# A fused decoder layer: the next head group's query, key and value projections moved into the present group's tail, and weight products in two sweeps

## The reference

```python
h = rmsnorm(x, g_pre_mix)
h_q, h_kv, h_pe, z, xbc, dt, gate_a, gate_b = split(h @ w_in)
q = rmsnorm(h_q, g_q) @ w_uq                # 16 heads, 64 + 32 rotary
c_kv, k_pe = rmsnorm(h_kv, g_kv), rope(h_pe)
k, v = c_kv @ w_uk, c_kv @ w_uv             # prompt; rows use the latents
o_attn = softmax(causal(q @ k) * scale) @ v
y, state = ssd_scan(silu(conv(xbc)), dt)    # 32 heads in 8 groups
o_ssm = rms_per_group((y + d_skip * x) * silu(z)) * g_ssm
merged = sigmoid(gate_a) * (o_attn @ w_br_attn) + sigmoid(gate_b) * (o_ssm @ w_br_ssm)
x = x + rmsnorm(merged @ w_out, g_post_mix)
x = x + rmsnorm(square(relu(rmsnorm(x) @ w_up)) @ w_down, g_post_mlp)
```

## Time and profile before

| | |
|---|---|
| median of three executions | 1900.58 us |
| the profiled execution, its own time | 1894.26 us |
| its span, first to last instruction | 1892.5 us |
| TensorE matmuls busy | 1616.1 us (85%), 11520 matmuls |
| VectorE busy | 998.0 us (53%) |
| ScalarE busy | 520.1 us (27%) |
| GpSimd busy | 477.8 us (25%) |
| mean granted TensorE clock | 0.916 of full speed |

### The profile page before, as it was taken

The page is one execution under the profiler, slowest core; times in us unless marked ns, Lnnn a source line. Parts: engine busy times, 40 slices in busy tenths (PEclk is TensorE's granted clock), DMA queues, the critical chain, the costliest instruction groups (busy, mean ns, idle before and its releaser), DMA issues.

```text
span 1892.5 us, 29047 instructions
## 1 busy us (share of the span) xinstructions
PE 1616.1 (85%) x11520; PEld 1391.9 (74%) x11520; DVE 998.0 (53%) x1780; ACT 520.1 (27%) x914; POOL 477.8 (25%) x196
## 2 busy tenths in 40 slices
PE   4788798788887888878876599999999499999995
PEld 4787687676877768777764346464799499999995
DVE  5568688686886868868685412121142622222225
ACT  3232323233232332333322112111222332222221
POOL 1232131221212212122120101111243444444441
PEclk9799899898898988989887799999899699999998
DMA  3132121221212212122130255564232122222221
GB/s 113 45 107 78 37 82 56 73 79 37 82 56 71 80 37 82 57 68 83 37 91 23 74 160 179 161 182 133 86 127 75 34 90 90 92 97 92 90 90 68
DMA packets 115738, 160.51 MB, mean 85 GB/s; under 512 B 18546, under 2 KB 89715, under 8 KB 115603
## 3 DMA queue, kind: packets, MB, share of 16 engines
q1 hardware_dynamic: 53714, 122.21, 20.4%
q10 hardware_dynamic: 61888, 36.44, 7.0%
HBM read 145.87 MB, written 12.74 MB: 84 GB/s over the span
## 4 chain that ended last, share of the span: by engine, by line
PE 60%; DVE 27%; issue 4%; ACT 3%; POOL 2%; DMA 1%; ACTq 1%; SPq 1%; DVEq 0%; POOLq 0%
PE lin L446 38%; PE Pb L664 3%; PE lin L684 3%; POOL w_lo L402 2%; PE Pb L464 2%; PE Pb L666 2%; PE lin L472 2%; DVE csm L1246 1%; DVE sm L1252 1%; DVE arena L1225 1%; PE lin L579 1%; PE Pb L520 1%; DVE acc L1421 1%; DVE arena L1357 1%; PE Pb L561 1%
## 5 line engine op out<-in xcount | busy, mean ns | idle before, releaser
L402 POOL TENSOR_TENSOR w_lo<-w_stage,w_hi 128x1024 fp32r<-128x1024 f32 x184 | 465.8, 2531 | 1365.4 <-ACT w_hi L778 1365.4
L446 PE MATMUL lin<-act_hi,w_hi 128*128 128x260 f32 x1760 | 370.4, 292 | 22.7 <-POOL w_lo L402 10.7
L446 PE MATMUL lin<-act_hi,w_lo 128*128 128x260 f32 x1760 | 358.1, 285 | 0.0
L446 PE MATMUL lin<-act_lo,w_hi 128*128 128x260 f32 x1760 | 357.6, 285 | 0.0
L778 ACT ACTIVATE w_hi<-w_stage 128x1024 fp32r<-128x1024 f32 x184 | 194.0, 1054 | 396.4 <-PE lin L446 366.3
L446 PEld LDWEIGHTS lin<-act_hi,w_hi 128*128 128x128 f32 x1760 | 275.5, 192 | 35.4 <-issue 16.3
L446 PEld LDWEIGHTS lin<-act_lo,w_hi 128*128 128x128 f32 x1760 | 275.9, 192 | 0.0
L446 PEld LDWEIGHTS lin<-act_hi,w_lo 128*128 128x128 f32 x1760 | 275.0, 191 | 0.0
L446 PE MATMUL lin<-mid_hi,w_hi 128*128 128x260 f32 x1024 | 220.0, 298 | 46.0 <-DVE acc L1421 20.8
L446 PE MATMUL lin<-mid_lo,w_hi 128*128 128x260 f32 x1024 | 214.2, 292 | 0.0
L446 PE MATMUL lin<-mid_hi,w_lo 128*128 128x260 f32 x1024 | 213.5, 291 | 0.0
(11 more groups left out here) (227 smaller groups left out, 2234.1 us busy)
## 6 DMA issues: line engine op xcount, KB each, us to landing
w_stage<-in_wall SPq DMA_DIRECT2D x184, 512.0 KB, 3.6
arena<-in_cache ACTq DMA_DIRECT2D x128, 128.0 KB, 2.8
arena<-in_state ACTq DMA_DIRECT2D x16, 512.0 KB, 8.0
out_stateT<-arena ACTq DMA_DIRECT2D x16, 512.0 KB, 4.1
arena<-in_cache SPq DMA_DIRECT2D x64, 128.0 KB, 2.3
o_attn<-in_cache SPq DMA_DIRECT2D x64, 128.0 KB, 2.3
arena<-in_xT SPq DMA_DIRECT2D x8, 520.0 KB, 5.4
out_yT<-arena SPq DMA_DIRECT2D x8, 260.0 KB, 2.0
```

What stands on the lines that cost most here:

```text
L402: pool.tensor_tensor(w_lo[:, slot, :], w_stage[:, slot, :], w_hi[:, slot, :].bitcast(F32), ALU.subtract).then_inc(S["w_split"], 1)
L446: mm = pe.matmul(lin[:, pl.slot, hf, 0:HALF], w[:, ch.slot, off:off + P], r[:, hf * HALF:(hf + 1) * HALF], start=(k == 0 and p == 0), stop ...
```

## The change

Two parts. First, the products uq0, uq1, uk, uv and ql of group i are issued in turn i in place of turn i+1: the queries between the scan and the statistics, keys and values between the statistics and the broadcast, the latent queries behind the broadcast. Turn 0 ends with all of them. ScalarE and VectorE evacuate them there too; `silu(0)` and the second z gate change place on VectorE; the weight chunks and PSUM slots are renumbered (bc, ql, s0 now follow each other, so s0 uses the slot of bc), and `rtmp` lies 16 columns further on. Second, `linear` waits for the high part of the weights alone, does both products with it over all tiles, then waits for the low part and does the third; `between` comes ahead of that second sweep.

```diff
--- before.py
+++ after.py
@@ -46,14 +46,14 @@
 
 
 IN_LIN = ["x0", "x1", "b", "c", "z0", "z1"]
-HEAD_LIN = ["uq0", "uq1", "uk", "uv", "ql", "bB"]
-TAIL_LIN = ["bc"] + [f"s{m}" for m in range(8)]
-FIRST_LIN = IN_LIN
-STEADY_LIN = HEAD_LIN + ["x0", "sA0", "x1", "bC", "sA1", "b", "sA2", "c", "sA3", "z0", "z1"] + TAIL_LIN
-LAST_LIN = HEAD_LIN + ["sA0", "bC", "sA1", "sA2", "sA3"] + TAIL_LIN
-FIRST_CH = IN_LIN
-STEADY_CH = ["UQ", "UKV"] + IN_LIN + ["SA", "SB"]
-LAST_CH = ["UQ", "UKV", "SA", "SB"]
+S_LIN = [f"s{m}" for m in range(8)]
+FIRST_LIN = IN_LIN + ["uq0", "uq1", "uk", "uv", "ql"]
+STEADY_LIN = (["bB", "x0", "sA0", "x1", "bC", "sA1", "b", "sA2", "c", "sA3", "z0", "z1", "uq0", "uq1", "uk", "uv", "bc", "ql"]
+              + S_LIN)
+LAST_LIN = ["bB", "sA0", "bC", "sA1", "sA2", "sA3", "bc"] + S_LIN
+FIRST_CH = IN_LIN + ["UQ", "UKV"]
+STEADY_CH = IN_LIN + ["UQ", "UKV", "SA", "SB"]
+LAST_CH = ["SA", "SB"]
 PRE_LIN = ["bcx", "misc", "q0", "q1", "q2", "kv0", "kv1", "bcq", "bckv"]
 PRE_CH = ["misc", "q0", "q1", "q2", "kv0", "kv1"]
 
...
@@ -432,23 +428,32 @@
 
 
                 if opens:
-                    pe.wait_ge(S["w_split"], ch.index + 1)
+                    pe.wait_ge(S["w_hi_done"], ch.index + 1)
                 free_slot(pl)
                 n = len(offs)
-                first = True
-                for k, (off, (rh, rl)) in enumerate(zip(offs, rhs)):
-                    if between and k == 3 * n // 4:
-                        between()
-                    if rhs_ready:
-                        pe.wait_ge(rhs_ready[0], rhs_ready[1] + (k + 1))
-                    for w, r, p in ((w_hi, rh, 0), (w_hi, rl, 1), (w_lo, rh, 2)):
+
+                def passes(k, of):
+                    off, (rh, rl) = offs[k], rhs[k]
+                    for w, r, p in of:
+                        r = (rh, rl)[r]
                         for hf in range(2):
                             mm = pe.matmul(lin[:, pl.slot, hf, 0:HALF], w[:, ch.slot, off:off + P],
                                            r[:, hf * HALF:(hf + 1) * HALF],
                                            start=(k == 0 and p == 0), stop=(k == n - 1 and p == 2))
-                            if first and opens:
+                            if opens and k == 0 and p == 0 and hf == 0:
                                 open_chunk(ch, mm)
-                            first = False
+                    return mm
+
+                for k in range(n):
+                    if rhs_ready:
+                        pe.wait_ge(rhs_ready[0], rhs_ready[1] + (k + 1))
+                    passes(k, ((w_hi, 0, 0), (w_hi, 1, 1)))
+                if opens:
+                    pe.wait_ge(S["w_split"], ch.index + 1)
+                if between:
+                    between()
+                for k in range(n):
+                    mm = passes(k, ((w_lo, 0, 2),))
                 mm.then_inc(S["lin_done"], 1)
 
             def act_rhs(n=KT):
@@ -508,9 +513,47 @@
                     if has_in:
                         linear(c_lin(i, name), c_chunk(i, name), K8, act_rhs(), between=between)
 
+                def queries():
+                    for h in range(2):
+                        linear(c_lin(i, f"uq{h}"), c_chunk(i, "UQ"), [k * 256 + h * P for k in range(3)],
+                               mid_rhs(0, 3), opens=(h == 0))
+
+                def keys():
+                    linear(c_lin(i, "uk"), c_chunk(i, "UKV"), [0, P], mid_rhs(3, 2))
+
+                def value_rows():
+                    ch, pl = c_chunk(i, "UKV"), c_lin(i, "uv")
+                    free_slot(pl)
+                    for c in range(NCH):
+                        for k in range(2):
...
+                    mm.then_inc(S["lin_done"], 1)
+
+                def latent_queries():
+                    ch, pl = c_chunk(i, "UKV"), c_lin(i, "ql")
+                    free_slot(pl)
+                    pe.wait_ge(S["lin_free"], c_lin(i, "uq1").index + 1)
+                    for k in range(2):
+                        out = lin[:, pl.slot, 0, 16 * k:16 * k + 16]
+                        for n, (w, r) in enumerate(((w_hi, qbd_hi), (w_hi, qbd_lo), (w_lo, qbd_hi))):
+                            mm = pe.matmul(out, w[:, ch.slot, 256 + k * P:384 + k * P], r[:, :],
+                                           start=(n == 0), stop=(n == 2))
+                    mm.then_inc(S["lin_done"], 1)
+
                 if not has_rest:
                     for name in IN_LIN:
                         project(name)
+                    pe.wait_ge(S["act_ready"], KT + 5)
+                    queries()
+                    keys()
+                    value_rows()
+                    latent_queries()
                     return
 
...
@@ -604,7 +620,7 @@
 
                 on_all("bB", 2)
                 pe.wait_ge(S["q_ready"], g * 2 + 2)
-                pe.wait_ge(S["lin_free"], c_lin(i, "uv").index + 1)
+                pe.wait_ge(S["lin_free"], c_lin(i - 1, "uv").index + 1)
                 scores(0)
                 project("x0")
                 for c in range(NCH):
@@ -626,11 +642,18 @@
                     if c < NCH - 1:
                         scores(u + 2)
                     values(u + 1)
+                if has_in:
+                    queries()
                 pe.wait_ge(S["o_ready"], g * 8 + 8)
                 pe.wait_ge(S["sqg_ready"], g * 2 + 2)
                 statistics(Pb[0:TOKT, 2, 0:8], sqg, 2).then_inc(S["g_stat"], 1)
+                if has_in:
+                    keys()
+                    value_rows()
                 pe.wait_ge(S["g_diag"], g + 1)
                 broadcast_stat(c_lin(i, "bc"))
+                if has_in:
+                    latent_queries()
                 for m in range(8):
                     linear(c_lin(i, f"s{m}"), c_chunk(i, "SA" if m < 4 else "SB"),
                            [(m % 4) * P, 512 + (m % 4) * P], mid_rhs(5, 2), opens=(m % 4 == 0),
@@ -866,6 +889,23 @@
                             else d["state"][:, 2 * t:2 * t + 2, :, :]
                         act.dma_start(sS[:, t], src.rearrange("b h p n -> (h p) b n")).then_inc(S[f"st_in{t}"], 16)
 
+                def heads_out():
+                    round_chunk(c_chunk(i, "UKV"))
+                    for h in range(2):
+                        pl = c_lin(i, f"uq{h}")
+                        done(pl)
+                        act.activation(cols(Qt[0:64, h, :]), lin_cols(pl, 0, 64), ACT.Copy)
+                        act.activation(qbd_hi[64 * h:64 * h + 64, 8 * h:8 * h + 8],
+                                       lin[0:64, pl.slot, 1, HALF - NB:HALF], ACT.Copy).then_inc(S["qbd_hi_s"], 1)
+                    pl = c_lin(i, "uk")
+                    round_chunk(c_chunk(i, "UKV").next())
+                    done(pl)
+                    act.activation(cols(Kt[0:64, 0, :]), lin_cols(pl, 0, 64), ACT.Copy).then_inc(S["k_act"], 1)
+                    pl = c_lin(i, "uv")
...
@@ -875,6 +915,7 @@
                     z_evac()
                     conv_tanh(3)
                     finish_inputs()
+                    heads_out()
                     return
 
                 def exponent(u):
...
@@ -1230,6 +1257,39 @@
                     dve.scalar_tensor_tensor(xc[:, k, :], xc[:, k, :], 1.0, cacc[:, k % 2, :], ALU.add, ALU.mult
                                              ).then_inc(S["xc_ready"], 1)
 
+                def queries_out(h):
+                    pl = c_lin(i, f"uq{h}")
+                    done(pl)
+                    link(dve.tensor_tensor(cols(rtmp[64:96, :]), lin_cols(pl, 96, 128), cols(ropet[96:128, :]), ALU.mult))
+                    link(dve.tensor_tensor(cols(Qt[64:96, h, :]), lin_cols(pl, 64, 96), cols(ropet[64:96, :]), ALU.mult))
+                    link(dve.tensor_tensor(Qt[64:96, h, :], Qt[64:96, h, :], rtmp[64:96, :], ALU.add))
+                    dve.wait_ge(S["qbd_hi_s"], i * 2 + (h + 1))
+                    dve.tensor_tensor(qbd_lo[64 * h:64 * h + 64, 8 * h:8 * h + 8],
+                                      lin[0:64, pl.slot, 1, HALF - NB:HALF],
+                                      qbd_hi[64 * h:64 * h + 64, 8 * h:8 * h + 8].bitcast(F32), ALU.subtract
...
@@ -1238,6 +1298,10 @@
                         conv(k)
                     z_gate((0, 1))
                     silu(3)
+                    queries_out(0)
+                    queries_out(1)
+                    keys_out()
+                    latents_out()
                     return
 
                 onehot = ident[0:32, bass.ds(g * 4, 4)]
...
@@ -1394,12 +1428,13 @@
                         conv(c - 1, 1)
 
                 if has_in:
-                    z_gate((0,))
+                    z_gate((0, 1))
+                    queries_out(0)
+                    queries_out(1)
                 dve.wait_ge(S["g_stat"], g + 1)
                 inverse_rms(Pb[0:TOKT, 2, 0:8], 0.25 / (D_INNER // GROUPS), S["g_diag"])
                 if has_in:
-                    z_gate((1,))
-                    silu(0)
+                    keys_out()
```

(8 more changed lines are left out.)

106 lines of the change are left out of this document (33 added, 73 removed).

## The result

The changed kernel takes 1924.22 us in the median of four executions, the kernel before 1898.18 beside it. Over all executions that is a ratio of 1.0147, 95% interval 1.0114 to 1.0181, slower by 1.5% where 0.6% faster was forecast. The profiled execution took 1927.41 us, its span is 1925.6. The first lines of the profile's page show no engine with more work to do: TensorE issues the same 11520 matmuls, and its busy share has not moved. Its busy time has grown with the span: 1639.2 us, where it was 1616.1, at a mean granted clock of 0.909 in place of 0.916.

What follows compares the result with a forecast made beforehand. No engine alone bounds the 119 us turn: TensorE works 102, waiting for VectorE and GpSimd. Seven turns at 1.0, front 3.7 and last head 1.0 give about 12 us won: 1888.6 us, range 1870 to 1903.

Steps and rivals of the forecast that it cites:

- (h): Head, L592 to the scan's L546, 10.85 us in the old kernel: VectorE still needs 10, gain 0.2 (-0.5 to +0.8).
- (d): Inverse root in the tail: GpSimd's low part of SA blocks VectorE for 2 us (0 to 2.5), ending at 478.9.
- (e): Broadcast from 479.0 taking 1.5 us, s0 waiting 0.68 more for its slot: s0 at 483.5, 8.6 later.
- A: The forecast: 5 to 20 us won, moved work mostly given back as the chain to s0 starts later; chance 0.55.
- B: Rival: the tail's hole is filled, the root not blocked or the clock staying up; 1875 us; chance 0.22.
- C: Rival: the move is worth nothing, only the sweeps count; 1894 to 1897 us; chance 0.13.
- D: Rival: between scan and statistics, queries run wholly at 1.2 GHz; 4.4 us a turn lost, 1920 us; chance 0.10.
- The sweeps: In `linear`, waits for GpSimd's low part go: 0.5 us a turn gained, 3.7 (2 to 6) in the front.
- (a): After the scan: uq0 needs z0's PSUM slot, queries stand ahead of statistics, first hole widened from 2.12 to 3.5 us.
- (b): Queries after the scan: 36 matmuls take 5.3 us with a cold start, ending at 470.6 (469.8 to 471.3).
- (c): Statistics behind dense work take 2.02 us, not 3.37, to 472.6; keys and values 4.5 us, to 477.1.
- (f): Output products: VectorE 1.65 us later by the s1 addition, +0.95 beyond s0's delay; s7 ends at 501.6, formerly 492.1.

Runs made afterwards that it cites:

- run a: The kernel before with the new `linear` alone, nothing moved: 1891.47 us against 1894.89, ratio 0.9970.
- run b: The changed kernel with the old `linear`, so the move alone: 1935.29 us, ratio 1.0201 to the kernel before.
- run d: The changed kernel with ScalarE rounding weight chunk SA later, behind the evacuation of the values: 1912.54 us, ratio 1.0088 to the kernel before.
- run f: The changed kernel with statistics and inverse root ahead of the queries and their evacuations: 1916.3 us, ratio 1.0094 to the kernel before.
- run c: The changed kernel with the decoding-state loads issued early, between the two query evacuations: 1909.66 us, ratio 1.0077 to the kernel before.
- run i: The kernel before with its decoding-state loads issued late, behind the evacuation of the values: 1935.56 us, ratio 1.0218 to the kernel before.
- e: The changed kernel with state loads issued early and SA rounded late: 1889.97 us against 1896.88 for the kernel before, ratio 0.9968.
- j: The changed kernel with state loads early, SA rounded late and the old `linear`: 1904.05 us, ratio 1.0038 to the kernel before.
- g: The changed kernel with state loads early, SA rounded late and statistics first: 1906.25 us, ratio 1.0040 to the kernel before.
- k: h with VectorE's convolution halves and `silu` spread among the output products' additions: 1878.35 us against 1895.72 for the kernel before, ratio 0.9897.
- h: The changed kernel reordered: statistics, uq0, broadcast, uq1; keys, values, latent queries between s3 and s4; state loads early; UKV behind SA: 1894.59 us, ratio 0.9975 to before.

## Why the prediction was wrong

The replay was off by 40 us: 12 won were forecast, 28 lost were measured by the ratio (26 by the medians). The step that failed is (h), the head: it gives the loads of the decoding states no price when the projections that cover them are moved away. Two more were mis-sized, the slot of the keys ahead of the broadcast in (d) and (e), and the middle of the turn, which was taken as unchanged.

The cases by name: the forecast A and its rivals B and C fail; D has the sign and, at 1920, nearly the time, but not the mechanism, so its nearness is luck. Its premise, queries and statistics wholly at 1.2 GHz, did not come: the queries took 5.7 us, at a mean granted clock of 0.74, and the statistics 2.00, at 1.00. The stretches are these (columns as in the earlier trace rows):

```profile
471.59:477.30 5.71, 5.71 (x36) 5.71 (x37) 2.35 (x4) 2.36 (x5) 2.38 (x1) 0.74 0.11 14
477.30:479.30 2.00, 2.00 (x35) 2.00 (x34) 1.87 (x5) 0.77 (x2) 0.00 (x0) 1.00 0.62 234
```

The lower end of the range is a small slip: B with the front at its best is 1873, not 1870. By steps:

- **The sweeps** held in the turns: z1's wait is gone in all of them, and run a's seven turns are 4.1 us shorter (3.5 written). The front's 3.7 is not shown: the waits are gone there too, but the first sdm product starts at 145.1 for 146.6, in run a at 146.7, and in run b, without the sweeps, at 144.7.
- **(a), (b), (c)** held: queries at 4.6 us after the scan (4.5 said), 5.7 us long (5.3), statistics 2.00 (2.02).
- **(d)** held, and was the step with the widest bounds: the root is cut by GpSimd for 2.2 us a turn (2 taken), shown by run d. The operation that was cut isn't one of the nine with two inputs that the step counted, but the `tensor_scalar` ahead of them (L1115). By the Trainium skill, page "SBUF — State Buffer", section "Who interferes with whom", the block was certain for an operation with two inputs; the trace of run f agrees, where L1118 took 2.23 us. But the step left out that the broadcast takes the slot of uk: it waits for VectorE's copy at L1278 too, 0.88 us more (486.54 for 485.66), since `keys_out` comes behind the root.
- **(e)** was right in the sum and wrong in its terms: the broadcast took 2.07 us for 1.5, and the 0.68 us for the slot did not come: s0 starts at 490.95, while the pair of subtractions at 490.10 runs to 491.47. That the two misses nearly cancel is luck.
- **(f)** held within 0.6: from s0 to the end of s7, 18.7 us (18.1).
- Together the tail is 2.1 us a turn longer than the replay's mean: 44.2, where 42.1 was the result of (g).
- **(h)** failed: "VectorE still needs 10: gain 0.2". It counts VectorE's operations between the sdm product and the scan and takes the states as there. The sentence on the queues looks at the weights, the history and `g_hi`, and not at the two `in_state` loads that ScalarE issues at the end of the tail. In the trace of before they left at 489.08 and were used at 505.05, 16 us later; a transfer takes 8.0 us. Taking 11.6 us of TensorE's work out from between leaves some 4.4, less than the transfer needs. The head became 12.1 us for 10.3 forecast, and by (h) the loads had no price at all. Run c gives 13 us back; run i makes the same loss in the old kernel, 41 us for 3.2 us of head and 1.9 of middle a turn.
- **The middle** was taken as unchanged but for the 0.5 us won at z1: 65.3; it was 67.2. That the low clock behind a new wait costs time in a stage that the change doesn't touch was priced in the tail only.
- **The last turn** was to gain 1.0 us. It took 65.9 us for 64.0, and between 61.8 and 68.7 in the other kernels: not resolved.

The profiled executions can be summed up: their spans differ by 33 us, 45 from the 12 won. Over the turns 1 to 7 the tail, the head and the middle are 36 us above the replay (15, 12 and 10), turn 8 is 3 and the front 2. The 4 us that are left lie behind the groups, where all kernels with the new sweeps have the same work and their profiled executions take from 844.7 to 854.9 us: scatter, as turn 8 and the front may be too.

The forecast of C, that the move itself is worth nothing, is near what runs e and j show once the two costs are off: e is level with the sweeps alone (0.9968 and 0.9970), j 0.4% worse than the kernel before. The prediction saw that the queries stood in the chain (a), and that the gain was given back; it did not ask what the work at the head had been hiding.

## What to carry to other kernels

Work that is moved away from a place had a cover to give: list the DMAs in flight and the waits of other engines across the stretch that it leaves, and move their issues with it. Filling a wait pays when the filler stands behind the instruction that starts the waited-for chain and in a buffer that is free by then; ahead of it, the filler lengthens the chain by its full time and by the wait for its own buffer: here the statistics came 7.2 us later, for queries of 5.7 us. Where another engine's long operation can block a chain, ask on each new order what it will fall on now: f and g moved the root away from one low part and under another. Two engines with nearly equal loads need their work interleaved finely: k differs from h only in where six pieces of VectorE's work stand (four halves of convolutions and two `silu`), and is 0.8% faster.

## What the runs showed of the hardware that was not expected

- The lock between VectorE and GpSimd isn't confined to operations with two SBUF inputs. The 65x8 `tensor_scalar` on integers, one input, stood for 2.37 us (0.17 in run d), and a 128x544 `tensor_scalar` (L1248) for 2.62 where it takes 0.56 alone:

```profile
492.82 2.62 DVE L1248 TENSOR_SCALAR arena<-arena,small 128x544 f32<-128x544 f32 x1
```

  The size of the operation played no part in these rows. The Trainium skill, page "SBUF — State Buffer", section "Who interferes with whom", has `tensor_scalar` among the operations that can take the port pair shared with GpSimd, when their operands meet certain conditions; the 2.37 and 2.62 us agree with it.
- A release on a `nop` of VectorE comes early. s0's slot is released by the `nop` behind the second subtraction, and s0 started about 0.5 us before that subtraction had ended. The Trainium skill, page "PSUM — Partial Sum Buffer", section "Engine vs sequencer instructions", says that an increment on a trailing `nop` is no completion signal, since the sequencer waits only for dispatch; the 0.5 us agree with it. My 0.68 us rested on the other reading.
- A wait of 5 us at the head was followed by 6 us at a granted clock of 0.57 and a first matmul of 2.07 us, for 1.12 in the earlier trace rows: the wait's price appears in the stage behind it, 1.4 us a turn on the mean.
